# First block's norms taken out of the projections' path: x times g split tile by tile, 1/rms applied afterwards

## What is computed

```
def rms_norm(x, g):
    y = x * lax.rsqrt(jnp.mean(x * x, axis=-1, keepdims=True) + 1e-6)
    return y * g
def hybrid_layer(h, pos, norm_g, w_in, ...):      # twice
    u = rms_norm(h, norm_g)
    dq, dk, dv, dz, fq, fk, fv, fz, f_logit = split(u @ w_in)
    # dq, dk: rotary (cos and sin tables), differential attention, per-head rms_norm
    # fq, fk, fv: attention with a forget gate: cumsum(log_sigmoid(f_logit + b_forget))
    mixed = concat([o_a * silu(dz), o_b * silu(fz)])
    return h + mixed @ w_out
first_block: h = layer 0, layer 1; return rms_norm(h, final_g)[:, 16:]
```

## Time and profile before

| | us |
|---|---|
| median of 3 runs | 1873.42 (1871.84 to 1873.96) |
| profiled execution, whole | 1873.47 |
| its span in the trace | 1871.7 |
| first block in it (to the first tile of the final norm, L1491) | 0 to about 426 |

### The profile page before, as it was taken

How to read it: one execution, slowest core, us unless ns; L and a number is a source line. 1 busy time by engine, 2 the same in 40 slices (tenths; PEclk the granted TensorE clock), 3 DMA queues, 4 the chain that set the end, 5 groups by cost and what they waited for, 6 DMA issues and landing times.

```text
span 1871.7 us, 27995 instructions
## 1 busy us (share of the span) xinstructions
PE 1737.7 (93%) x10004; PEld 1503.7 (80%) x10004; DVE 1397.9 (75%) x1545; ACT 1160.5 (62%) x1306; POOL 227.6 (12%) x230
## 2 busy tenths in 40 slices
PE   5998799988789999887999999999999999999994
PEld 4887698877789998876888888888888888888883
DVE  5655466637765556865889888888888988988886
ACT  5554355545454445654777777777777777777774
POOL 0212022104500000700001000010010100100000
PEclk9999999998899999987999999999999999999997
DMA  6322333143345444343999999999999999999994
GB/s 262 136 80 69 136 136 111 51 160 133 108 163 182 165 156 173 137 153 118 365 369 370 362 366 384 375 368 372 370 372 368 359 380 383 371 356 375 375 372 167
DMA packets 71335, 477.44 MB, mean 255 GB/s; under 512 B 8405, under 2 KB 9077, under 8 KB 19285
## 3 DMA queue, kind: packets, MB, share of 16 engines
q1 hardware_dynamic: 67637, 463.25, 66.2%
q0 software_dynamic: 3328, 12.08, 1.7%
q10 hardware_dynamic: 288, 1.05, 0.1%
HBM read 470.05 MB, written 6.29 MB: 255 GB/s over the span
## 4 chain that ended last, share of the span: by engine, by line
PE 80%; DVE 6%; issue 6%; ACT 4%; POOL 2%; DMA 1%; SPq 0%; DVEq 0%; ACTq 0%; POOLq 0%
PE bank L420 25%; PE bank L422 24%; PE bank L421 24%; ACT whi L406 2%; DVE wlo L411 1%; PE bank L528 1%; PE bank L963 1%; POOL cacc L1857 1%; DVE rstd L1306 1%; DVE msb L1482 1%; PE bank L646 1%; ACT sq L1021 0%; DVE ut L1311 0%; PE bank L935 0%; POOL py L1841 0%
## 5 line engine op out<-in xcount | busy, mean ns | idle before, releaser
L411 DVE TENSOR_TENSOR wlo<-raw,whi 128x2048 fp32r<-128x2048 f32 (+2 forms) x454 | 1009.5, 2228 | 239.4 <-ACT whi L406 237.9
L406 ACT ACTIVATE whi<-raw 128x2048 fp32r<-128x2048 f32 (+2 forms) x454 | 845.2, 1863 | 241.7 <-PE bank L422 239.8
L420 PE MATMUL bank<-whi,hthi 128*128 128x512 f32 x896 | 358.4, 400 | 0.0
L422 PE MATMUL bank<-whi,htlo 128*128 128x512 f32 x896 | 354.1, 395 | 0.0
L421 PE MATMUL bank<-wlo,hthi 128*128 128x512 f32 x896 | 353.9, 395 | 0.0
L420 PE MATMUL bank<-uhi,whi 128*128 128x272 f32 (+2 forms) x1072 | 319.7, 298 | 20.5 <-DVE ulo L1323 20.2
L422 PE MATMUL bank<-uhi,wlo 128*128 128x272 f32 (+2 forms) x1072 | 311.1, 290 | 0.0
L421 PE MATMUL bank<-ulo,whi 128*128 128x272 f32 (+2 forms) x1072 | 310.6, 290 | 0.0
L420 PEld LDWEIGHTS bank<-uhi,whi 128*128 128x128 f32 (+1 forms) x1072 | 207.3, 193 | 24.5 <-issue 22.2
L421 PEld LDWEIGHTS bank<-ulo,whi 128*128 128x128 f32 (+1 forms) x1072 | 207.6, 194 | 0.6
L422 PEld LDWEIGHTS bank<-uhi,wlo 128*128 128x128 f32 (+1 forms) x1072 | 207.0, 193 | 0.0
(11 more groups left out here) (294 smaller groups left out, 2098.7 us busy)
## 6 DMA issues: line engine op xcount, KB each, us to landing
raw<-in_wm SPq DMA_DIRECT2D x338, 1024.0 KB, 7.1
raw<-in_w SPq DMA_DIRECT2D x66, 1024.0 KB, 4.8
raw<-in_w SPq DMA_DIRECT2D x18, 768.0 KB, 4.0
raw<-in_w SPq DMA_DIRECT2D x16, 704.0 KB, 3.9
raw<-in_w SPq DMA_DIRECT2D x14, 512.0 KB, 3.5
ys<-y_slots SPq DMA_DIRECT2D x4, 512.0 KB, 5.2
raw<-in_w SPq DMA_DIRECT2D x2, 576.0 KB, 3.6
h_in<-in_hT SPq DMA_DIRECT2D x1, 1088.0 KB, 9.6
```

The costliest lines, as they stand in the source:

```text
L406: act.activation(whi[:, n % RING, 0:c], raw[:, n % RAW, 0:c], ACT.Copy).then_inc(hi_ready, 1)
L411: dve.tensor_tensor(wlo[:, n % RING, 0:c], raw[:, n % RAW, 0:c], whi[:, n % RING, 0:c].bitcast(F32), ALU.subtract).then_inc(lo_ready, 1)
L420: pe.matmul(out, s_hi, m_hi, start=start, stop=False, skip_group_check=shared)
L422: return pe.matmul(out, s_lo, m_hi, start=False, stop=stop, skip_group_check=shared)
```

## The change

**Norm.** `uhi` and `ulo` are now the two parts of h g, without 1/rms. ScalarE makes `uhi` (`tile_hi`) and the square (`tile_square`) of a tile in turn, VectorE makes `ulo` in one operation (`tile_lo`). GpSimd adds the squares up in `acc` (`square_adds`, seven additions), and TensorE sums over features once (`square_sum`), behind feature tile 5 of the first two output tiles. In layer 0 this is done straight from the loaded x; for layer 1 and for the final norm it is done at the end of the layer before, tile by tile, behind each addition to `hT`.

**1/rms.** It is applied afterwards. For the rotary heads' q and k (8 of the 33 tiles) VectorE scales the two sine tables and GpSimd the two cosine tables once a layer (`roper`); ScalarE still takes those tiles. The other 25 tiles are now taken out of their bank by VectorE, with the multiplication by `rstd` (`take_scaled`), at the start of slot s. ScalarE computes tanh and the logit chain from what VectorE wrote.

**Start.** Unit 0 is loaded first, then gains and x in two halves straight into `hT`; the load of the lambda vectors comes after the tables, and their exponentials move to slot 2.

```
+            def tile_hi(q, k):
+                act.activation(uhi[:, k, :], hT[:, k, :], ACT.Copy, scale=gain).then_inc(uhi_ready, 1)
+            def tile_square(q, k):
+                if k >= 2:
+                    act.wait_ge(acc_step, q * (KD - 1) + max(k - 2, 1))
+                act.activation(sq[:, k % 2, :], hT[:, k, :], ACT.Square).then_inc(sq_ready, 1)
...
             act.wait_ge(const_ready, 1)
+            act.activation(warm[:, 0:1], eps[:], ACT.Sqrt)
             split_hi(act, 0)
+            act.wait_ge(in_landed, 16)
+            for k in range(KD):
+                act.wait_ge(x_landed[k // (KD // 2)], 16)
+                tile_hi(0, k)
+                tile_square(0, k)
             split_hi(act, 1)
             with act.Fori(0, LAYERS) as l:
-                norm_squares(l, LEN, hT, x_ready, 1, l * KD)
-                norm_hi(l, LEN)
                 split_hi(act, 2, l, U1)
+                root(l)
...
-                for u in range(PROJ_U + 1, U1):
-                    split_hi(act, u + 2, l, U1, UNITC if u + 2 >= U1 else None)
+                act.activation(warm[:, 1:2], eps[:], ACT.Sqrt)
+                for u in range(PROJ_U, U1):
+                    if u > PROJ_U:
+                        split_hi(act, u + 2, l, U1, UNITC if u + 2 >= U1 else None)
+                    for d in out_tiles(u):
+                        act.wait_ge(x_ready, l * KD + (d + 1))
+                        tile_hi(l + 1, d)
+                        tile_square(l + 1, d)
+            root(2)
...
+            def tile_lo(q, k):
+                dve.wait_ge(uhi_ready, q * KD + (k + 1))
+                dve.scalar_tensor_tensor(ulo[:, k, :], hT[:, k, :], gain, uhi[:, k, :].bitcast(F32), ALU.mult, ALU.subtract).then_inc(ulo_ready, 1)
+            def scaled_tables(l):
+                norm_scale(l)
+                for i in (1, 3):
+                    dve.tensor_tensor(roper[:, i, :], rope[:, i, :], rstd[:], ALU.mult).then_inc(sin_ready, 1)
+            def take_scaled(l, i):
+                dve.wait_ge(*tile_done(l, i))
+                if kind == "z":
+                    op = dve.tensor_tensor(zs[:, g, :], src, rstd[:], ALU.mult)
...
             with dve.Fori(0, LAYERS) as l:
-                norm_split(l, l, hT, LEN)
                 split_lo(dve, 2, l, U1)
+                scaled_tables(l)
                 for s in range(SLOTS):
+                    if s < PROJ_T:
+                        take_scaled(l, s)
                     turned(l, s - 1)
...
                     for d in out_tiles(u):
                         dve.tensor_tensor(hT[:, d, :], hT[:, d, :], out_bank(d)[:, 0:LEN], ALU.add).then_inc(x_ready, 1)
+                        if d:
+                            tile_lo(l + 1, d - 1)
...
+            def square_adds(q):
+                for k in range(1, KD):
+                    pool.wait_ge(sq_ready, q * KD + (k + 1))
+                    pool.tensor_tensor(acc[:], acc[:] if k > 1 else sq[:, 0, :], sq[:, k % 2, :], ALU.add).then_inc(acc_step, 1)
```

More of the change, by code:

```diff
@@ L52 @@
         TILE_OF[_b + _j] = (_kind, _g)
+RAW_TAKEN = {i: 2 * g + (kind == "k") for i, (kind, g) in TILE_OF.items() if kind in ("q", "k") and g < DIFF_HEADS}
+SCALED_TAKEN = {i: j for j, i in enumerate(i for i in range(PROJ_T) if i not in RAW_TAKEN)}
+RAWS, SCALED = len(RAW_TAKEN), len(SCALED_TAKEN)
 OUT_SLOTS = 4
@@ L195, in build_program @@
         rstd = sb("rstd", [P, LEN])
+        acc = sd
         gated = ExitStack()
@@ L251, in build_program @@
         lame = sb("lame", [P, LAYERS, 2], scope=first)
-        lamd = sb("lamd", [P, LAYERS], scope=first)
+        lam0 = sb("lam0", [P, LAYERS], scope=first)
         lam = sb("lam", [P, LAYERS], scope=first)
-        xb, ab, lf, le, ll = (logits[:, i, :] for i in range(5))
+        xb, ab, lf = (logits[:, i, :] for i in range(3))
         first.close()
@@ L340, in build_program @@
         in_landed, par_landed = sem("in_landed"), sem("par_landed")
+        x_landed = [sem(f"x_landed{i}") for i in range(2)]
+        acc_step, ms_done, cos_ready, sin_ready = sem("acc_step"), sem("ms_done"), sem("cos_ready"), sem("sin_ready")
+        raw_taken, scaled_taken, tanh_ready = sem("raw_taken"), sem("scaled_taken"), sem("tanh_ready")
         lam_landed, par2_landed = sem("lam_landed"), sem("par2_landed")
@@ L523, in _, with square_sum @@
         def _(pe):
+            def square_sum(q):
+                pe.wait_ge(acc_step, q * (KD - 1) + (KD - 1))
+                pe.matmul(bank[7][:, 0:LEN], mean_d[:], acc[:], start=True, stop=True).then_inc(ms_done, 1)
             def norm_sums(q, n):
@@ L1051, in take_tile @@
+                    act.wait_ge(logit_step, 4 * l + 1)
                     act.activation(ab, xb, ACT.Abs).then_inc(logit_step, 1)
[L1052 to L1061, removed]
+                    act.wait_ge(logit_step, 4 * l + 2)
@@ L1334, in _ @@
             dve.memset(one[:], 1.0).then_inc(const_ready, 1)
+            split_lo(dve, 0)
+            for k in range(KD):
+                tile_lo(0, k)
+            split_lo(dve, 1)
             dve.wait_ge(lam_landed, 32)
@@ L1375, in log_forget @@
                     key_cum(l, f)
+            def scaled_tables(l):
+                norm_scale(l)
+                dve.wait_ge(par_landed, 16 * N_PAR)
+                for i in (1, 3):
+                    dve.tensor_tensor(roper[:, i, :], rope[:, i, :], rstd[:], ALU.mult).then_inc(sin_ready, 1)
+                dve.wait_ge(sin_ready, 2 * l + 2)
+            def take_scaled(l, i):
+                if i not in SCALED_TAKEN:
+                    return
+                kind, g = TILE_OF[i]
+                src = bank[i % 2][:, 0:LEN]
+                dve.wait_ge(*tile_done(l, i))
+                if kind == "z":
+                    op = dve.tensor_tensor(zs[:, g, :], src, rstd[:], ALU.mult)
+                elif kind == "logit":
+                    op = dve.tensor_tensor(xb, src[0:FOX_ROWS, :], rstd[0:FOX_ROWS, :], ALU.mult)
+                elif kind == "v":
+                    if g >= 2:
+                        dve.wait_ge(vt_done, l * VN + (g - 1))
+                    op = dve.tensor_tensor(vt[:, g % 2, :], src, rstd[:], ALU.mult)
+                else:
+                    dve.wait_ge(s_done, l * MAPS + 2 * (g - 1))
+                    op = dve.scalar_tensor_tensor(qk[:, 2 * (g % 2) + (kind == "k"), :], src, -SCALE if kind == "q" else 1.0, rstd[:],
+                                                  ALU.mult, ALU.mult)
+                op.then_inc(scaled_taken, 1)
             def turned(l, i):
@@ L1813, in _ @@
                             op.then_inc(fox_p, 1)
+                square_adds(l + 1)
             pool.wait_ge(xs_ready, KD)
```

139 lines of the change are left out of this document (78 added, 61 removed).

## The result

The changed kernel takes 1878.47 us (median of 16 runs, 1873.98 to 1881.47) against 1873.42 for the kernel before: a ratio of 1.0025, 95% interval 1.0017 to 1.0033, so 3.2 to 6.2 us slower. One of the 16 executions of the kernel before took 3450.61 us; it does not move the median. The 5.05 us between the medians are over the 0.2% (3.7 us) that the prediction set as the smallest difference to be told from none, though the lower end of the interval is not. 1878.47 lies inside the stated range of 1864 to 1883 and 0.5 us above the upper bound (1878) that the prediction's own terms gave. The profiled execution took 1878.85 us with a span of 1877.0, 5.3 us above the span before.

The account below looks back on a forecast made before the run. TensorE was taken to bound the layers' body, but not the start, seam and end. Heads, body and end summed as -7.2 - 0.8 + 1.8 + 6.9 = +0.7 us, median 1874.1; terms' bounds 1870.5 to 1878, stated range 1864 to 1883.

Parts of the forecast that it names:

- first head: Layer 0's start up to tile 4's first matmul: earlier projections, then VectorE's queue sets the pace; -7.2 us.
- body, layer 0: Layer 0 after the head: VectorE's added takes delay the logit chain, an old stall swallows tile 27's new wait; +0.9 us.
- seam and second head: End of layer 0 up to tile 4 of layer 1: five-operation chain paces additions, ScalarE's jump on the path; -0.8 us.
- body, layer 1: Layer 1 after its head: same logit delay and swallowed tile 27 wait as in layer 0; +0.9 us.
- the end: End of layer 1 to the final norm: the five-operation chain costs more than dropping the old norm saves; +6.9 us.
- not swallowed: Tile 27 in both layers: the old stall moves along with the new wait, 5.0 us lost a layer, 1882.3; chance 0.32.
- third rival: Layer 1's end: TensorE paces the additions as before, making the last term -1.7 and the total 1856.8; chance 0.04.
- TensorE's lead carries through: Both heads: worth all TensorE gains on tiles 0 and 1, 13.4 and 5.2 us, giving 1863.5; chance 0.22.
- The seam's chain is shorter: Layer ends: TensorE paces additions as before; last term -1.7, second -9.5, giving 1856.8; chance 0.04.
- no change within 0.2%: Whole kernel: the likeliest case, +0.7 us, within the 3.7 us a measurement cannot tell from none; chance 0.42.

Follow-up runs that it names:

- run 1: Changed kernel with ScalarE's uhi and square of an output tile moved behind the next unit's high part: 1863.46 us, ratio 0.9952 to the kernel before.
- run 2: Changed kernel with ScalarE's loop over the two layers written out: 1877.31 us, ratio 1.0024 to the kernel before.
- run 3: Changed kernel with VectorE's last per-head reciprocal moved behind the take of tile 27: 1876.10 us, ratio 1.0022 to the kernel before.
- run 5: Changed kernel with the loops over the two layers written out on ScalarE and VectorE: 1872.67 us, ratio 0.9998 to the kernel before.
- run 6: Changed kernel with uhi and square lagging one unit, and loops written out on TensorE, VectorE, ScalarE and GpSimd: 1855.91 us, ratio 0.9907 to the kernel before.
- run 7: Changed kernel with lagged uhi and square, later last reciprocal, shorter logit chain and four loops written out: 1854.98 us, ratio 0.9900 to the kernel before.
- run 8: Changed kernel with the logit chain starting at the absolute value with bias, the biased copy made two tiles later: 1877.72 us, ratio 1.0025 to the kernel before.
- run 4: Changed kernel with GpSimd's additions of squares 2 to 7 cut to one column each, for timing only: 1874.61 us in one run.
- run 9: Kernel before the change with loops written out on TensorE, VectorE, ScalarE and GpSimd: 1870.72 us, ratio 0.9986 to the kernel before.
- run 10: Changed kernel with SyncE's order of loads at the start as before the change: 1886.05 us, ratio 1.0073 to the kernel before.

## Why the prediction came out as it did

The forecast was +0.7 us, within 0.2%; measured is +5.0, interval +3.2 to +6.2. Each term against the profile, as the lead at one event and the next:

| term | predicted | profile |
|---|---|---|
| first head | -7.2 | -8.7 |
| body, layer 0 | +0.9 | +2.7 |
| seam and second head | -0.8 | +1.6 |
| body, layer 1 | +0.9 | +2.7 |
| the end | +6.9 | +7.2 |
| sum | +0.7 | +5.6 |

*The first head*: the mechanism was right up to the start of tile 3 (VectorE's queue, not TensorE). For tile 4 it held where the low clock was short: in runs 1 to 3 and 5 to 7 the scores follow VectorE's `qk` within 0.3 us. In the changed kernel's own profile and in run 8 TensorE's tile 3 at the low clock came last, by 1.5 and 1.1 us; the prediction had no such term here. The row of `tile_lo` and additions was mis-sized: "8 x 0.50 + 7 x 0.77 = 9.4 us" were 7.0 (9.77 to 16.76). The first addition began beside the low part of unit 0. The other six took 0.79 us each and started every 0.93, and the `tile_lo` beside them took about 1.0 each where they take 0.50 without an addition (run 4). So the operations do hold each other up, but a pair costs 0.93 and not the 1.27 of the sum; why, no run here shows. Run 4 shows that some half a microsecond of those six reaches the path, because ScalarE's 0.73 us a tile, which the sum left out, comes next behind them. The rule of the Trainium skill ("SBUF — State Buffer", "SBUF: two separate sides") on the shared port pair fits the rows: an addition that started beside a low part took 2.17 us (run 1) and one with VectorE idle 0.78. The rule held for these and had little weight here.

*The seam and the second head* failed on one number. "ScalarE now has a jump back to the loop's start on the path: 1.67 us of issue" was 4.98, 3.3 us more. The 1.67 were what was left to see behind a 1.9 us high part; behind a 0.4 us square most of the jump shows. That the high part covered the rest is my reading: 1.92 + 1.67 = 3.6 is less than 0.41 + 4.98 = 5.4, and no run explains the difference. Runs 2 and 5 show both the jump and that a second one, of 4.82 us, lay behind it. The word "hidden before" was wrong too, as run 9 shows. The rest of this term held: additions 3.53 and 5.45 us apart for 3.6 and 5.5, and the last square ended at 220.8 for 221.2 (the predicted 227.1 less the lead of 5.94).

*The body* was mis-sized, +2.7 for "+0.9" in both layers, and this is the largest miss. From the scores before tile 4 to the first addition it took 157.4 us before in both layers. In the seven profiles whose instructions there are those of the changed kernel (its own and runs 1, 2, 4, 5, 6 and 10) it took 159.4 to 161.0 in layer 0 and 159.2 to 162.0 in layer 1, so +1.8 at the least and about +3 on average. The take of tile 27 made the wait of 3.7 us as predicted, and the old `pr` stall swallowed most of it, but not all: the lead went from 6.52 to 5.93 over the stretch in layer 0 (0.6 lost) and from 3.31 to 1.63 in layer 1 (1.7 lost, with eight matmuls at the low clock behind the wait). I had counted nothing for it. Run 3 confirms the swallowing, so the rival "not swallowed" falls as a mechanism, and its 1882.3 with it. But the line that the prediction drew for it, +2.4 us a layer, was reached: the loss came from the smaller form of that rival and from the logit tile together. At the logit tile the chain itself cost 1.1 us for 0.9: TensorE waited another 0.55 us for `qraw` ahead of the 2.59 for `pr`. In layer 0 it then also ran its transposes at the low clock, where they ran at the high one before, and the low clock lasted 18 projection matmuls for 15: 1 us more. That microsecond can't be laid to the change: in layer 1 it is missing (a lead of 3.49 us at the transposes and at the scores behind them), and in runs 2 and 9 no low clock followed that wait at all. The prediction had the clock only in its bounds, +1.7 a layer, and both layers came out above them.

*The end* was right within 0.3 us, and run 1 shows its cause: with the chain loosened the last term turns from +7.2 into -1.6, where the prediction's third rival had -1.7.

*TensorE's lead carries through* falls: TensorE had tiles 0 and 1 done at 19.81, 14.5 us earlier than before, and only 8.7 were left at tile 4. *The seam's chain is shorter* was no result of this change, but run 1 made it so by one reordering and measured 1863.5, with the jumps still in it (1855.9 without them in run 6, 1856.8 in that rival).

So the sum came out near partly by luck: a better head (-1.5) offset part of three costs that were too small (+3.6 in the body, +2.4 at the seam, +0.3 at the end). The total missed by 4.3 us, and the likeliest case, no change within 0.2%, did not come true. The stated range held it because it reached out to both rivals.

## What to carry to other kernels

When work is put between the stages of a pipeline of splits, look at which engine's next job ahead of the pipeline now stands behind it: here two 0.4 us operations ahead of high parts of 1.05 and 1.9 us cost 15 us in two places, and the same work behind it made the change pay. A loop's jump is a cost that each engine pays for itself (seen here on three), visible in full only where nothing long runs ahead of it, and a second engine's jump shows only when the first is gone. Of two waits fed by the same queue, add the pair before counting one of them.

## What the runs showed of the hardware

On three engines the jump back in these loops showed as 4 to 5 us of issue when the instruction ahead of it was short: ScalarE 4.98 behind a 0.41 us square (4.33 in run 1, 4.72 to 5.05 in runs 3, 4, 8 and 10), VectorE 4.82 behind a 0.50 us `tile_lo` (run 2), and TensorE 4.05 ahead of its first matmul of layer 1 (run 3):

```profile
214.67 0.39 PE L429 MATMUL bank<-uhi,whi 128*128 128x272 f32 x1 [4.05 <-issue]
```

Behind a 1.92 us high part 1.67 us showed. GpSimd's and SyncE's jumps were not seen.

The stretch of low clock behind one and the same wait differs from profile to profile. Behind TensorE's wait ahead of tile 3, two kernels with the same start, the changed one and run 5 (columns: length, busy PE, PEld, DVE, ACT, POOL, granted clock, DMA share, GB/s):

```profile
28.03:33.02 4.99, 4.99 (x24) 4.99 (x24) 3.98 (x5) 0.00 (x0) 0.34 (x1) 0.51 0.44 143
```
```profile
27.88:29.90 2.02, 2.02 (x11) 2.02 (x10) 2.02 (x2) 0.00 (x0) 0.44 (x1) 0.51 0.81 333
```

Both are at a granted clock of 0.51, 1.2 of 2.4 GHz, but one lasts 4.99 us and the other 2.02. That moves the scores before tile 4 from 32.08 to 33.54. Behind the 2.6 us wait at the logit tile the changed kernel ran 18 projection matmuls at 0.50, run 5 ran 14, and run 2 stayed at 1.00. So a single profile tells the size of such a term only within some 1.5 us.
